# Low-rank decay columns of an input projection: high and low weight halves loaded together as 64 stationary columns, summed by a 65-row product

## The reference, cut to what matters

```python
N_IN = 14 * W_GRP + 2 * GATE_RANK          # W_GRP 256, GATE_RANK 16
hN = rms_norm(x, norm_g_l) * (1.0 + scale) + shift
p = hN @ w_in_l
(qA, kA, vA, gA, bB, cB, hB, gB, uC, gC, qD, kD, vD, gD, aF, aB) = split_in(p)
...
la_f = to_heads(jax.nn.log_sigmoid((aF @ up_f + b_f)) / GLA_TAU, N_HEADS_D)
la_b = to_heads(jax.nn.log_sigmoid((aB @ up_b + b_b)) / GLA_TAU, N_HEADS_D)
```

## Time and profile before

| | us |
|---|---|
| median of 3 runs | 2787.53 (2783.85 to 2796.4) |
| the profiled execution's own time | 2787.69 |
| its span in the profile | 2786.0 |
| PE busy | 2554.9 (92%) |
| DVE, ACT, POOL busy | 1257.1, 990.5, 740.5 |

### The profile page before, as it was taken

The page is one execution under the profiler, slowest core; times in us unless marked ns, Lnnn a source line. Parts: engine busy times, 40 slices in busy tenths (PEclk is TensorE's granted clock), DMA queues, the critical chain, the costliest instruction groups (busy, mean ns, idle before and its releaser), DMA issues. The chain is left out here.

```text
span 2786.0 us, 53595 instructions
## 1 busy us (share of the span) xinstructions
PE 2554.9 (92%) x19228; PEld 2056.2 (74%) x19228; DVE 1257.1 (45%) x2620; ACT 990.5 (36%) x2031; POOL 740.5 (27%) x1145
## 2 busy tenths in 40 slices
PE   3899999999999949999999997999899952999999
PEld 1788888888888838888888875777777741888887
DVE  2444343443443343323323325667667722566555
ACT  2444444444444342222222214555555621111110
POOL 2223233233332310000000004333233321444442
PEclk8999999999999979999999998999999976999999
DMA  7433333333333254223223218887677667766664
GB/s 289 144 106 119 110 114 122 102 118 118 107 119 107 84 184 140 93 81 96 92 81 97 92 52 170 179 180 170 144 154 168 153 151 235 244 202 213 209 203 135
DMA packets 271822, 395.35 MB, mean 142 GB/s; under 512 B 43270, under 2 KB 192678, under 8 KB 269628
## 3 DMA queue, kind: packets, MB, share of 16 engines
q1 hardware_dynamic: 258396, 368.21, 46.3%
q10 hardware_dynamic: 12735, 24.07, 2.5%
q0 software_dynamic: 544, 1.09, 0.2%
HBM read 267.31 MB, written 125.96 MB: 141 GB/s over the span
## 5 line engine op out<-in xcount | busy, mean ns | idle before, releaser
L258 PE MATMUL p_ps_m<-p_w_hi,p_h_hi 128*128 128x512 f32 x1904 | 771.8, 405 | 21.1 <-DVE p_h_lo L823 21.1
L260 PE MATMUL p_ps_m<-p_w_hi,p_h_lo 128*128 128x512 f32 x1904 | 750.4, 394 | 0.0
L259 PE MATMUL p_ps_m<-p_w_lo,p_h_hi 128*128 128x512 f32 x1904 | 750.3, 394 | 0.0
L258 PEld LDWEIGHTS p_ps_m<-p_w_hi,p_h_hi 128*128 128x128 f32 x1904 | 359.7, 189 | 99.6 <-issue 21.8
L260 PEld LDWEIGHTS p_ps_m<-p_w_hi,p_h_lo 128*128 128x128 f32 x1904 | 358.9, 189 | 80.7
L259 PEld LDWEIGHTS p_ps_m<-p_w_lo,p_h_hi 128*128 128x128 f32 x1904 | 360.1, 189 | 73.3
L258 PE MATMUL o_ps_y<-o_w_hi,o_y_hi 128*128 128x512 f32 x544 | 217.5, 400 | 9.7 <-DVE o_y_lo L1784 9.7
L260 PE MATMUL o_ps_y<-o_w_hi,o_y_lo 128*128 128x512 f32 x544 | 217.4, 400 | 0.0
L259 PE MATMUL o_ps_y<-o_w_lo,o_y_hi 128*128 128x512 f32 x544 | 215.7, 397 | 0.0
L537 POOL TENSOR_TENSOR p_ve<-p_ss,p_eps 128x1 f32<-128x1 f32 x68 | 12.9, 190 | 601.1 <-ACT p_xr L603 601.1
L814 DVE TENSOR_TENSOR p_xt<-p_xt,p_ps_r 128x1024 f32<-128x1024 f32 x68 | 82.7, 1216 | 193.0 <-PE p_ps_r L714 193.0
(11 more groups left out here) (217 smaller groups left out, 4512.6 us busy)
## 6 DMA issues: line engine op xcount, KB each, us to landing
a_scan<-s_scan SPq DMA_DIRECT2D x68, 258.0 KB, 5.7
s_scan<-p_w_raw SPq DMA_DIRECT2D x136, 128.0 KB, 2.4
a_kv<-s_kv SPq DMA_DIRECT2D x68, 256.0 KB, 6.3
a_v_win<-s_p SPq DMA_DIRECT2D x132, 128.0 KB
p_xr<-in_x_sample SPq DMA_DIRECT2D x32, 512.0 KB, 4.0
p_xt<-in_x_sample_t SPq DMA_DIRECT2D x32, 512.0 KB, 4.7
p_xr<-in_x_columns SPq DMA_DIRECT2D x32, 512.0 KB, 10.1
p_xt<-in_x_columns_t SPq DMA_DIRECT2D x32, 512.0 KB, 10.8
```

Of the source, the lines that this page charges most:

```text
L258: pe.matmul(out, left_hi(k), right_hi(k), start=(k == 0), stop=False)
L259: pe.matmul(out, left_hi(k), right_lo(k), start=False, stop=False)
L260: last = pe.matmul(out, left_lo(k), right_hi(k), start=False, stop=(k == K8 - 1))
```

## The change

The 32 high columns and the 32 low columns of the decay weights now stand side by side in an array of their own, `w_a`, 64 columns wide; `w_hi` and `w_lo` lose them (2048 columns each). Per slice one product takes all 64 columns with the high part of the tokens, one takes the 32 high columns with the low part. The low weights' sum lands on partitions 32 to 63 and is no longer added in PSUM: `aug` becomes 65 rows (64 sums and the ones), and `up` repeats both gate matrices on rows 32 to 63, so the gate product adds them.

```diff
-        w_hi = sb("w_hi", [P, K8, width], F32R)
-        w_lo = sb("w_lo", [P, K8, width], F32R)
+        if which == 0:
+            w_a = sb("w_a", [P, K8, 4 * RANK], F32R)
+        kept = width - 2 * RANK if which == 0 else width
+        w_hi = sb("w_hi", [P, K8, kept], F32R)
+        w_lo = sb("w_lo", [P, K8, kept], F32R)
+
+        def halves(k, nk, wd, a0):
+
+            if wd == 2 * RANK:
+                return w_a[:, k:k + nk, 0:wd], w_a[:, k:k + nk, wd:2 * wd]
+            at = a0 - 2 * RANK if kept < width and a0 >= 1024 else a0
+            return w_hi[:, k:k + nk, at:at + wd], w_lo[:, k:k + nk, at:at + wd]
...
-            up = sb("up", [2 * RANK + 1, 2, W_GRP])
-            aug = sb("aug", [2 * RANK + 1, P])
+            up = sb("up", [4 * RANK + 1, 2, W_GRP])
+            aug = sb("aug", [4 * RANK + 1, P])
...
-                    pool.dma_start(up[d * RANK:(d + 1) * RANK, d, :], io[w].rearrange("a r n -> (a r) n")).then_inc(up_in, 16)
-                    pool.dma_start(up[2 * RANK:2 * RANK + 1, d, :], io[b]).then_inc(up_in, 16)
+                    for part in range(2):
+                        at = (2 * part + d) * RANK
+                        pool.dma_start(up[at:at + RANK, d, :], io[w].rearrange("a r n -> (a r) n")).then_inc(up_in, 16)
+                    pool.dma_start(up[4 * RANK:4 * RANK + 1, d, :], io[b]).then_inc(up_in, 16)
...
-                act.activation(w_hi[:, k:k + nk, a0:a0 + wd], w_raw[n % 4][:, 0:nk * wd].rearrange("p (k n) -> p k n", k=nk),
+                act.activation(halves(k, nk, wd, a0)[0], w_raw[n % 4][:, 0:nk * wd].rearrange("p (k n) -> p k n", k=nk),
...
-                pe.wait_ge(up_in, 64)
+                pe.wait_ge(up_in, 96)
...
-                        product(pe, ps_m[g][0:b - a, 0:P], lambda k: w_hi[:, k, a:b], lambda k: w_lo[:, k, a:b],
-                                lambda k: h_hi[s][:, k, :], lambda k: h_lo[s][:, k, :]).then_inc(mm, 1)
+                        for k in range(K8 - 1):
+                            pe.matmul(ps_m[g][0:4 * RANK, 0:P], w_a[:, k, :], h_hi[s][:, k, :], start=(k == 0), stop=False)
+                        for k in range(K8):
+                            pe.matmul(ps_m[g][0:2 * RANK, 0:P], w_a[:, k, 0:2 * RANK], h_lo[s][:, k, :], start=False, stop=False)
+                        pe.matmul(ps_m[g][0:4 * RANK, 0:P], w_a[:, K8 - 1, :], h_hi[s][:, K8 - 1, :], start=False, stop=True).then_inc(mm, 1)
                         return
+                    if kept < width and g > G_A:
+                        a, b = a - 2 * RANK, b - 2 * RANK
...
-                    dve.tensor_copy(aug[0:2 * RANK, :], ps_m[G_A][0:2 * RANK, 0:P]).then_inc(aug_done, 1)
+                    dve.tensor_copy(aug[0:4 * RANK, :], ps_m[G_A][0:4 * RANK, 0:P]).then_inc(aug_done, 1)
```

More of the change, by code:

```diff
@@ L527, in _ @@
                 pool.wait_ge(consts, 6)
-                pool.memset(aug[2 * RANK:2 * RANK + 1, :], 1.0).then_inc(consts, 1)
+                pool.memset(aug[4 * RANK:4 * RANK + 1, :], 1.0).then_inc(consts, 1)
                 pool.wait_ge(consts, 7)
@@ L837, in _ @@
                 dve.wait_ge(w_hi_done, n + 1)
-                dve.tensor_tensor(w_lo[:, k:k + nk, a0:a0 + wd], w_raw[n % 4][:, 0:nk * wd].rearrange("p (k n) -> p k n", k=nk),
-                                  w_hi[:, k:k + nk, a0:a0 + wd], ALU.subtract).then_inc(w_lo_done, 1)
+                high_part, low_part = halves(k, nk, wd, a0)
+                dve.tensor_tensor(low_part, w_raw[n % 4][:, 0:nk * wd].rearrange("p (k n) -> p k n", k=nk),
+                                  high_part, ALU.subtract).then_inc(w_lo_done, 1)
             if which == 0:
```

## The result

| | before | after |
|---|---|---|
| median | 2786.98 us (2783.85 to 2796.4, 4 runs) | 2743.18 us (2740.1 to 2745.23, 4 runs) |
| profiled execution, its span | 2787.69, 2786.0 | 2740.1, 2738.4 |
| PE busy | 2554.9 | 2517.5 |

The ratio is 0.984, 95% interval 0.9817 to 0.9863: 43.8 us less, where 26.1 were forecast.

What follows compares the result with a forecast made beforehand. The prediction took PE, busy without a wait in tiles 1 to 32, as the bound. Narrow products 13.5 plus gate product rows 12.6 made 26.1 us, so 2787.69 - 26.1 = 2761.6 us, range 2750 to 2775.

Steps and rivals of the forecast that it cites:

- Place of the weights: First projection stage: 3264 wide products read from other addresses; put at nothing, with 16 us either way as ends.
- wide products at another step than 0.232 us: Sign that the forecast is wrong: products of 512 moved columns no longer cost 0.232 us each.
- Narrow products: `G_A`: 24 products become 16, eight of them 64 wide at 0.069 us; 13.5 us saved (10.9 to 15.8).
- The exposed load behind the last narrow product: Out of `G_A`: a 128-column weight load leaves 0.058 us exposed; scaled to 64 columns it gave 0.069 us.
- Rows of the gate product: Gate product: 65 rows instead of 33 remove a 0.37 us gap in 34 tiles; 12.6 us saved (0 to 12.6).
- Tile 0: First tile: PE waits 8.7 us for DVE's weight splitting, so fewer narrow products gain nothing there.
- The keys: Nearest condition crossing tiles: POOL has them 4.6 us before PE wants them, so no engine takes over.
- The two more DMAs at the start: POOL's queue: 0.98 us fits in 2.57 us of idle time; without that cover, 0.98 us once.
- Rival 1: `G_A`: each change of stationary width stops PE, costing 12.2 us; 13.9 us left, 2773.8 us; chance 0.06.
- Rival 2: Gate product: 65 rows keep the gap, only the narrow products gain; 2774.2 us; chance 0.08.
- rival 3: The saved time comes back as a wait on keys, norms or stores; about 2787 us; chance 0.05.
- rival 4: `G_A`: a 64-column load cannot run ahead, 0.200 us per product; 8.5 us slower, 2796.2 us; chance 0.04.

Runs made afterwards that it cites:

- e1_layout: The kernel before the change with only the decay columns moved out of `w_hi` and `w_lo` into two 32-column arrays; 2773.14 us, ratio 0.9956.
- e3_pitch2064: The changed kernel with 16 unused columns behind each row of `w_hi` and `w_lo`; 2754.67 us, ratio 0.9895 against the kernel before.
- e2_rows65: The kernel before the change with only `aug` and `up` made 65 rows instead of 33, the added `up` rows zero; 2770.6 us, ratio 0.9942.

## Why the forecast was wrong, step by step

**The step that failed is "Place of the weights".** It saw that 3264 wide products read from other addresses, saw that their step can be 0.231 or 0.226 us, and put the difference at nothing, "as both occur with one layout". That was a wrong conclusion from a right row. That one layout shows both values does not say that all layouts do: in the stage of the earlier trace rows the step falls to 0.226 within a group, and in the stage of the change it did not (231.8 to 232.6 ns in the later half of every group from the second tile on), which the 22 steps of 0.232 in the earlier trace rows already hinted at. In the built program before, the rows of `w_hi` are 8320 bytes apart, so that in every other slice the moved operand is 128 bytes off; afterwards they are 8192 apart. The step fell to 226.7 ns in the later part of each group. The mean over all of a group is 3.8 ns less, and 3.8 x 96 x 34 is 12.4 us. `e1_layout` has it alone (11.8 us less), `e3_pitch2064` takes it away (11.5 us back). The text's own ends of 16 us either way did hold the term; the range took in only a part of them. With the whole of it below the forecast's lower end of 2759.3 the range would have begun at 2743.3, beside the 2743.18 measured. The text also named this sign of being wrong, wide products at another step than 0.232 us, and it came.

**Narrow products: right mechanism, size at the end of its range.** The term was 13.5 us with 0.069 us for a 64-wide product. From the last wide product, 523.48, to the first 32-wide one, 524.58, it is 1.10 us: one wide step (0.227), four transposes at 0.1115 and seven 64-wide products, which leaves 0.061 for each of these. The eight 32-wide ones take 0.47 us (524.58 to 525.05), 0.059 each. So the price of the lower end was right, the 64-column load adds at most 0.002 us to a step, and the term is 15.8 us. The exposed load behind the last narrow product, from which 0.069 was scaled, was no measure for a load between equals.

**Rows of the gate product: right.** 0.385 us a tile instead of 0.37, 13.1 us instead of 12.6. `e2_rows65` has it alone. By the medians over the tiles half of it goes at the entry (from the last transpose to the second instruction of the gate product, 0.416 us before and 0.223 after), half at the exit (from the last of them to the second wide product, 0.538 and 0.345).

**The rest held.** Tile 0 still waits for DVE, a little longer (8.7 us before); waits view of PE, 60 to 118 us:

```profile
PE p_ps_q L790 <- DVE p_rows L886: 9.3, 1, 9.3
```

The keys are ready on POOL at 519.26 and PE wants them at 523.72, a slack of 4.46 us, 0.16 less than before:

```profile
517.84 1.42 POOL L566 TENSOR_TENSOR p_w_raw<-p_w_raw,p_dq 128x256 f32<-128x256 f32 x2
```

The two more DMAs at the start do not hold POOL up, which still waits 1.54 us behind them for ACT (2.57 before):

```profile
52.56 0.19 POOL L550 TENSOR_TENSOR p_ve<-p_ss,p_eps 128x1 f32<-128x1 f32 x1 [1.54 <-ACT p_xr L616]
```

The stage's first wide product does start a little later, 19.37 us behind POOL's first instruction of the stage instead of 19.05. It is 19.0 in `e1_layout` and `e2_rows65`, which have the old number of DMAs, and 19.3 to 19.6 in the runs with two more. That is some 0.3 us once, and by which path is not shown.

**The corrected sum** is 15.8 + 13.1 + 12.4 = 41.3 us. The profile shows 39.2 up to the next stage. Of the 2.1 us between them some 0.5 is steps counted twice, 0.6 tile 0's longer wait for DVE and 0.3 the later first product; 0.7 is left over. The medians differ by 43.8.

**The rivals.** Rival 1, that each change of stationary width stops PE, is refuted: the 1.10 us just counted hold the changes from 128 to 64 and from 64 to 32 columns and leave nothing over, and the way out, 525.05 to 525.40, is 0.35 us as before. The Trainium skill, TensorEngine Tiling (Array Packing), section Key Properties, says that a change of the tiling mode drains TensorE. These runs agree where the number of rows in use goes from 128 to 33 and back, with a loss of some 0.19 us each time. They show no loss where the columns go from 128 to 64 to 32, although the built program marks these products with array parts of their own, 128 by 64 and 128 by 32. Rival 2 is refuted by `e2_rows65`, rival 3 by the windows row, rival 4 by the 0.061 us. None of the rivals contained the layout, although the text named it; it was treated as an uncertainty and not as a mechanism with a price.

## What to carry to other kernels

When an edit changes the width or the order of arrays, look at the step of the products that read them, before and after, even if they are not part of the edit: 3.8 ns on 3264 products, 12.4 us, was nearly as much as either intended saving (15.8 and 13.1). In a float32r stage with a weight load for every product, try placing the stationary and the moved operand a multiple of 256 bytes apart, row pitches included: it gave the fast step wherever it was tried in this kernel, and a pad of 352 bytes gave 10 us in a stage that the change did not touch. And when a row shows two values of a size within one layout, ask why it has the better one, and where, before taking it as noise.

## What was not expected of the hardware

- A product of 512 moved float32r columns behind a load of 128 stationary ones costs 226.7 ns in the later half of a group if the two operands begin a multiple of 256 bytes apart in every slice, and 228.9 to 233.5 ns in the cases tried where they do not. In the first projection stage, where the granted clock is 1.00 on both sides, `e1_layout` shows it without any other change. Where each begins made no difference at the places tried (768, 800 and 896 modulo 1024 were equally fast). The Trainium skill, SBUF — State Buffer, section Operand start alignment, asks only for a start at a multiple of the element size and says that its own runs timed nothing; the runs here add a time.
- Why distance counts is open; no run here shows it. Nor is it each product for itself: before the change the operands of every other slice were a multiple of 256 bytes apart, and the steps of a group's last four slices were 232.2 ns in each.
- Even with the right distance most groups of both projection stages begin with 4 to 9 steps of about 230 ns (behind the group's first) before the step is 226.7. No run here explains that.
- The number of stationary columns, 32 or 64, makes no difference between moves of 128 columns: 0.060 and 0.061 us.
